# Moving three adaLN groups out of the expert routing in a four-layer diffusion step

## What is computed

```
mod = (silu(c) @ w_ada[i] + b_ada[i]).reshape(.., 6, D_MODEL)        # per layer i
h = rmsnorm(x, norm_mix[i]) * (1 + mod[1]) + mod[0];  x = x + mod[2] * mixer(h)
h = rmsnorm(x, norm_ffn[i]) * (1 + mod[4]) + mod[3];  x = x + mod[5] * moe(h)
moe: scores = sigmoid(h @ w_router); best group of four experts; two experts a token;
     y = sum_e combine[e] * (silu(h @ wg[e]) * (h @ wu[e])) @ wd[e]
```

## Time and profile before

| what | value |
|---|---|
| runs | 1558.07, 1559.05, 1563.91 us; median 1559.05 |
| the profiled execution | 1560.72 us, span 1558.6 us, 22820 instructions |
| TensorE (PE) busy | 1258.2 us, 81% of the span; granted clock 0.901 of full speed |
| VectorE, ScalarE, POOL busy | 362.8, 304.7, 165.8 us |
| DMA | 420.59 MB moved, mean 270 GB/s |
| queue q1 (SP's weights) | 331.37 MB, 54.3% of the 16 engines' span |
| queue q0 (POOL's) | 85.90 MB, 14.3% |
| chain that ended last | PE 60%, DMA 22%, VectorE 6%, issue 5%, POOL 3% |

### The profile page before, as it was taken

How to read it: one execution, slowest core, us unless ns; L and a number is a source line. 1 busy time by engine, 2 the same in 40 slices (tenths; PEclk the granted TensorE clock), 3 DMA queues, 4 the chain that set the end, 5 groups by cost and what they waited for, 6 DMA issues and landing times.

```text
span 1558.6 us, 22820 instructions
## 1 busy us (share of the span) xinstructions
PE 1258.2 (81%) x9738; PEld 729.6 (47%) x9738; DVE 362.8 (23%) x1127; ACT 304.7 (20%) x672; POOL 165.8 (11%) x231
## 2 busy tenths in 40 slices
PE   4889865799998999955798898889995567698756
PEld 2445432457865556522376433354652225464324
DVE  1442100230025234100121122223410004621003
ACT  1231100221136231100132112113110003311103
POOL 3001121200000000131200000000013120012210
PEclk8899987899999999987898999789998787899878
DMA  9999997933257758998741247605899875179952
GB/s 323 420 421 419 420 388 290 357 111 108 84 201 281 298 190 317 419 418 340 261 174 67 81 151 291 260 27 202 317 419 419 346 312 220 41 278 419 391 217 93
DMA packets 93266, 420.59 MB, mean 270 GB/s; under 512 B 12692, under 2 KB 38792, under 8 KB 52073
## 3 DMA queue, kind: packets, MB, share of 16 engines
q1 hardware_dynamic: 68048, 331.37, 54.3%
q0 software_dynamic: 24112, 85.90, 14.3%
q10 hardware_dynamic: 1000, 1.80, 0.3%
HBM read 418.93 MB, written 25.86 MB: 285 GB/s over the span
## 4 chain that ended last, share of the span: by engine, by line
PE 60%; DMA 22%; DVE 6%; issue 5%; POOL 3%; ACT 2%; SPq 1%; POOLq 0%; another core or an unknown queue 0%; ACTq 0%; DVEq 0%
PE bank L423 56%; DMA sb_ring<-in_w_exp_up,sb_spare 6%; DMA sb_ring<-in_w_exp_down,sb_spare 5%; DMA sb_ring<-in_w_exp_up 3%; POOL sb_ring L1963 2%; DMA sb_ring<-in_w_ada 2%; DMA sb_arena<-slot_out,sb_slots 2%; DMA slot_out<-sb_arena,sb_homes 1%; PE bank L868 1%; PE bank L800 1%; DMA sb_arena<-in_k_band 1%; POOL sb_arena L1984 1%; DMA sb_arena<-token_rows,sb_rows 1%; DVE sb_arena L1797 1%; SPq L410 1%
## 5 line engine op out<-in xcount | busy, mean ns | idle before, releaser
L423 PE MATMUL bank<-sb_ring,sb_arena 128*32 128x256 f32 (+1 forms) x5792 | 452.5, 447 | 152.8 <-DMA sb_ring<-in_w_exp_down,sb_spare 64.6
L423 PEld LDWEIGHTS bank<-sb_ring,sb_arena 128*32 128x32 f32 x5792 | 214.0, 115 | 360.7 <-issue 176.9
L423 PE MATMUL bank<-sb_arena 128*128 128x128 f32 (+8 forms) x600 | 110.6, 336 | 10.6 <-DVE sb_arena L1726 6.2
L423 PE MATMUL bank<-sb_ring,sb_hT 128*128 128x256 f32 x528 | 116.4, 383 | 2.6 <-ACT sb_hT L1087 2.6
L423 PE MATMUL bank<-sb_ring,sb_cond 128*2 128x512 f32 x768 | 102.0, 660 | 13.1 <-DMA sb_ring<-in_w_ada 12.3
L423 PEld LDWEIGHTS bank<-sb_ring,sb_hT 128*128 128x128 f32 x528 | 101.0, 192 | 17.9 <-issue 3.2
L423 PEld LDWEIGHTS bank<-sb_arena 128*128 128x128 f32 (+1 forms) x600 | 86.4, 203 | 37.7 <-issue 9.9
L1790 DVE TENSOR_TENSOR sb_arena<-sb_arena,bank 128x256 f32<-128x256 f32 x36 | 15.2, 421 | 345.2 <-PE bank L423 345.2
L423 PE MATMUL bank<-sb_arena,sb_ring 128*128 128x384 f32 (+2 forms) x288 | 94.3, 504 | 0.9 <-ACT sb_arena L1141 0.9
L423 PE MATMUL bank<-sb_hT,sb_ring 128*128 128x384 f32 x256 | 83.0, 486 | 0.7 <-DVE sb_hT L1608 0.7
L1797 DVE COPY sb_arena<-bank 128x512 f32<-128x512 f32 x36 | 24.9, 691 | 196.4 <-PE bank L423 196.4
...
## 6 DMA issues: line engine op xcount, KB each, us to landing
...
```

Source lines behind the costliest of these rows:

```text
L423: return pe.matmul(out, lhsT, rhs, start=first, stop=last)
```

## The change

The table `ADA_WINDOW` goes. Groups 3 and 7 (`ADA_TAIL`) are loaded behind the experts' units of layers 0 and 1 and multiplied in `combine`: four units between the products of the last round's outputs and the wait for the gathered rows, four behind the last of the 24 transposing products, in front of the next norm. Their transposes come behind that norm, the copy on ScalarE behind its squares, `mod_columns` ahead of VectorE's norm. Group 11 (`ADA_LATE`) is loaded behind layer 2's experts and multiplied in layer 3: four units at the start of the pooling mixer (behind the wait for `mix_in`), two behind the mixer, two and the transposes behind the second norm; group 2 of layer 0 keeps its place. Bank 7 stays with adaLN, so `combine` has seven banks: the eighth chunk shares bank 2 with the second, and its first product waits until VectorE has used that chunk (`x_ready`). `hold` moves on by eight units (`KC`) in all layers.

```diff
@@ -317,3 +317,4 @@
         ADA_MIXER = [(), (4, 5, 6), (8, 9, 10), ()]
-        ADA_WINDOW = [(3,), (7,), (11,), ()]
+        ADA_TAIL = [3, 7, None, None]
+        ADA_LATE = [2, None, None, 11]
         hold = {}
@@ -323,4 +324,3 @@
             if kind == 0:
-                if L == 0:
-                    ada_units(2)
+                ada_units(ADA_LATE[L])
             elif kind == 1:
@@ -348,6 +348,5 @@
             n_y += 8
-            ada_units(*ADA_WINDOW[L])
             moe_first.append(len(units))
 
-            hold[len(units) + 3 * (NE + SPARES) + 6] = (yg_in[NT - 1], 32 * (L + 1))
+            hold[len(units) + 3 * (NE + SPARES) + 6 + KC] = (yg_in[NT - 1], 32 * (L + 1))
 
@@ -371,2 +370,4 @@
             down_units(ROUNDS - 1)
+            if ADA_TAIL[L] is not None:
+                ada_units(ADA_TAIL[L])
 
@@ -380,3 +381,3 @@
 
-        COMBINE = [6, 2, 3, 1, 0, 7, 4, 5]
+        COMBINE = [6, 2, 3, 1, 0, 4, 5, 2]
 
@@ -536,2 +537,3 @@
                 else:
+                    ada(ADA_LATE[3], 0, 1, 2, 3)
                     project_group(r, 0)
@@ -832,5 +834,2 @@
                 ins.then_inc(pos_full, 1)
-                for g in ADA_WINDOW[L]:
-                    ada(g, 4, 5, 6, 7)
-
                 pe.wait_ge(slots_ready, 5 * L + 2)
@@ -848,5 +847,2 @@
                 ins.then_inc(pos_full, 1)
-                for g in ADA_WINDOW[L]:
-                    ada_columns(g)
-                    pe.wait_ge(mod_added, g + 1)
                 assert state["u"] == moe_first[L]
@@ -910,7 +906,16 @@
                     pe.wait_ge(ya_ready, R + ROUNDS)
-                    for c in (1, 2, 3, 0, 4, 5, 6, 7):
-                        if c == 0:
-                            pe.wait_ge(yb_ready, R + ROUNDS)
+                    def upper(c):
                         mm(bank[c][:, 0:TOK], ysb[:, 0, c * P:(c + 1) * P], last_a, True, False)
+
+                    for c in (1, 2, 3):
+                        upper(c)
+                    pe.wait_ge(yb_ready, R + ROUNDS)
+                    for c in (0, 4, 5, 6):
+                        upper(c)
+                    if ADA_TAIL[L] is not None:
+                        ada(ADA_TAIL[L], 0, 1, 2, 3)
                     for c in range(KC):
+                        if c == KC - 1:
+                            pe.wait_ge(x_ready, 8 * (n + 1) + 2)
+                            upper(c)
                         for t in range(NT):
@@ -920,2 +925,4 @@
                         ins.then_inc(yc_full, 1)
+                    if ADA_TAIL[L] is not None:
+                        ada(ADA_TAIL[L], 4, 5, 6, 7)
 
@@ -996,2 +1003,4 @@
                     norm(2 * L)
+                    if ADA_TAIL[L - 1] is not None:
+                        ada_columns(ADA_TAIL[L - 1])
                 (pool_mixer, mlstm, mla)[L % 3](2 * L)
@@ -1000,9 +1009,9 @@
                 if L == 0:
-                    ada(2, 0, 1, 2, 3, 4, 5)
+                    ada(2, 0, 1, 2, 3)
+                if ADA_LATE[L] is not None:
+                    ada(ADA_LATE[L], 4, 5)
                 norm(2 * L + 1)
-                if L == 0:
-                    ada(2, 6, 7)
-                    ada_columns(2)
-                for g in ADA_WINDOW[L]:
-                    ada(g, 0, 1, 2, 3)
+                if ADA_LATE[L] is not None:
+                    ada(ADA_LATE[L], 6, 7)
+                    ada_columns(ADA_LATE[L])
                 experts(L, 2 * L + 1)
@@ -1066,3 +1075,3 @@
 
-            def norm_scale(n):
+            def norm_scale(n, late=None):
                 if n and n % 2 == 0:
@@ -1074,2 +1083,4 @@
                     act.activation(sq[:, 2 * k:2 * k + 2, :], xT[:, 2 * k:2 * k + 2, :], ACT.Square).then_inc(sq_ready, 1)
+                if late is not None:
+                    mod_rows(late)
                 act.wait_ge(ms_full, n + 1)
@@ -1268,4 +1279,2 @@
                 tokens(0)
-                for g in ADA_WINDOW[L]:
-                    mod_rows(g)
                 silu(0)
@@ -1302,3 +1311,3 @@
                 if L:
-                    norm_scale(2 * L)
+                    norm_scale(2 * L, ADA_TAIL[L - 1])
                 act.wait_ge(mod_added, 3 * L + 1)
@@ -1312,4 +1321,4 @@
                 norm_scale(2 * L + 1)
-                if L == 0:
-                    mod_rows(2)
+                if ADA_LATE[L] is not None:
+                    mod_rows(ADA_LATE[L])
                 act.wait_ge(mod_added, 3 * L + 2)
@@ -1754,4 +1763,2 @@
                                        op0=ALU.add, op1=ALU.add).then_inc(slots_ready, 1)
-                for w in ADA_WINDOW[L]:
-                    mod_columns(w)
                 eq = rt[:, 20, :]
@@ -1871,2 +1878,4 @@
                 kind = L % 3
+                if L and ADA_TAIL[L - 1] is not None:
+                    mod_columns(ADA_TAIL[L - 1])
                 norm(2 * L, amp[:, L, 0, :, :])
@@ -1881,4 +1890,4 @@
                     mod_columns(ADA_MIXER[1][2])
-                if L == 0:
-                    mod_columns(2)
+                if ADA_LATE[L] is not None:
+                    mod_columns(ADA_LATE[L])
                 norm(2 * L + 1, amp[:, L, 1, :, :])
```

## The result

The changed kernel takes 1596.54 us (median of 4 runs, 1593.25 to 1598.91) where the kernel before, beside it on the same chip, takes 1558.56: a ratio of 1.0231, 95% interval 1.0196 to 1.0265, so 36 us slower. The profiled execution took 1596.69 us with a span of 1594.7, 36.1 more than before. The forecast was 1595. Its terms came out less exactly than their sum, and the rows show it. One execution of all that follow, of the version with the hold alone, took 2163.9 us at a mean granted clock of 0.549; the ratios leave it out, and why it was long stays open.

The account below looks back on a forecast made before the run. The prediction took DMA engines to bound expert stretches and TensorE with its helpers the mixers. Its terms summed to +35.6 us on the 1559.05 us median, 1594.7, rounded to 1595, with a range of 1570 to 1611.

Parts of the forecast that it names:

- What bounds the kernel: Whole kernel: DMA engines bound expert stretches, TensorE and its helpers bound mixers; the weight ring is full before the gate product.
- C: Behind layers 0 and 1: four adaLN units in front of the next norm add in full, twice, +7.6 us.
- D: Combine, all four layers: the eighth chunk's late product stands on the path, 0.67 us each, +2.7 us.
- A: Layer 0's experts: their stream starts with the ring full, as layer 3's does, -7.0 us; bounds -20 and 0.
- B: Last gathers of layers 0, 1, 2: more weight loads share the engines with them, +22.7 us (+4.3, +6.2, +12.2).
- E: Routing of layers 1 and 2: the 60 products run at the slow clock without adaLN work before them, +4.0 us.
- F: Layer 3's tables: loaded with the DMA engines to themselves, they arrive sooner, -2.6 us.
- G: Layer 3: group 11's units at the mixer's start and around the second norm are not hidden, +8.2 us.
- Gather last: Last gathers: they wait until all twelve weight units are through, +53 us in all, 1612 us; chance 0.12.
- hold harmless: Last gathers: the moved hold costs nothing, +13 us, 1572; chance 0.09, or 0.07 with layer 0's full gain, about 1559.
- weight queue decides: Everywhere: the weight queue sets the time and TensorE's work is hidden, -26.6 us, 1532 us; chance 0.06.
- rival 4: Combine: moved groups arrive late and TensorE waits for them, up to 10 us; given no chance of its own.

## Why the prediction was right

**What bounds the kernel** held: the ring was full before the first gate product in layers 0 and 1 (rows above), and adaLN products in front of a norm moved it by about their length (C and D).

**A** (layer 0's experts): forecast -7.0, measured +1.1 - 9.2 = -8.1. One profile flatters it, though. Over all profiles the stream takes 137.1 to 141.8 us with the group in front (mean 139.0 of six) and 127.6 to 137.1 without (mean 132.9 of seven), so the stream gains nearer 6 than 9 us, and A is nearer -5. The bound of -20 was far away. The spread among the seven has a place: the spare experts' up matrices, which POOL asks for 69.5 to 71.5 us into the stream, are used 92.1 to 96.3 us into it where it takes 127.6 to 132.4 us, and 100.0 to 101.4 us where it takes 135.3 to 137.1. Why they land later there stays open.

**B** (the last gather): forecast +22.7, measured +27.7 (6.1, 6.5, 15.2 against 4.3, 6.2, 12.2). The mechanism is shown three ways: the hold alone makes it, the hold put back removes it, the hold closed turns its sign. This is the term that was mis-sized. 3.4 of the 5.0 us are the stores ahead of the gather, which I left out: the gather's first instruction comes 22.1 us behind the down products in layer 0 instead of 19.1, half of that layer's loss, and 0.5 us later in layer 1. The gather itself (first instruction to last row) grew by 3.1, 6.0 and 15.2 us, so layer 2 is 3.0 over the forecast and layer 0 1.2 under. In layer 2, from 1297 to 1321 us, q1 sent 887 packets beside the gather's 861, where I had 818. That isn't more bytes (6.40 MB, and I had 6.7): I had counted 8.2 KB for each packet of a load, but 144 packets make a load of 1 MiB, 7.3 KB each. With that the same working would give layer 2 +11.1 and B about 21, further from what was measured. What the 22 us left out is an end below full rate: from 1315 to 1321 us 1.87 MB moved, 312 GB/s, where I had 420 GB/s to the last row.

**C and D**: forecast 7.6 + 2.7. Measured +4.5 in layer 0 and +4.2 in layer 1 (4.5 each forecast), +0.6 in layer 3; putting the units in the wait returned 3.7 and 3.5 of it, and the banks alone cost 0.6 to 0.8 a layer. In layer 2, where only D applies, last row to norm took 16.7 us against 16.8: its 0.7 us doesn't show in this profile.

**E** (routing clock): forecast 2.0 each in layers 1 and 2, measured 1.2 and 0.8. The start at clock 0.50 was right, and so was the cause, since products that keep the clock take it away. But I took layer 3's distance for both, 9.65 us from the start of the 60 products to the first expert product, where 9.37 and 8.41 were measured. In layer 2 that is the whole shortfall: the 60 products took 8.48 us, not 9.72. In layer 1 they took 9.44, with the clock back at 0.81 in their second half, and began 0.5 us sooner behind the norm (22.3 us instead of 22.9).

**F** (layer 3's tables): forecast -2.6, measured -2.8. From POOL's request to the products it takes 7.15 us, not 9.88. More weights beside the tables than before lengthen them by 6 us, which is the same mechanism from the other side.

**G** (group 11 in layer 3): forecast +8.2, measured +5.4. At the front the four units took 5.05 us, but the 24 products behind them 5.45 instead of 7.93: +2.6, where I had +3.8. I had charged 3.8 at full clock and credited nothing more, which was one row too coarse. Two units in front of the second norm cost their 1.9. For the two behind it I charged 2.5 us; VectorE's norm starts 7.0 us later, but the first expert product only 5.4: the 60 products begin 21.0 us behind the norm instead of 22.0 and take 9.12 us, not 9.72.

**Not forecast:** layer 2's mixer, +5.7 us. It needn't be the change's. The same stretch takes 287.9 us in the kernel before, 294.4 in the version that differs from it in layer 3 alone, and 285.6 to 293.6 in the others. Windows of 20 us, 230 us into that mixer, of the kernel before,

```profile
1020.34:1040.34 20.00, 15.32 (x47) 9.43 (x47) 4.71 (x14) 2.32 (x6) 0.00 (x0) 0.83 0.00 1
```

of the changed kernel,

```profile
1033.93:1053.93 20.00, 15.46 (x38) 9.52 (x38) 3.97 (x12) 2.32 (x6) 0.00 (x0) 0.55 0.00 1
```

and of the version with 12 products in layer 3,

```profile
1019.96:1039.96 20.00, 15.47 (x36) 9.15 (x35) 3.96 (x12) 2.32 (x6) 0.00 (x0) 0.52 0.00 1
```

show the granted clock at 0.83, 0.55 and 0.52 with the same idle share. Which level a profile meets there changes from one execution to the next, and what decides it stays open.

**The sum.** A to G measured come to 33.6 us, against 35.6 forecast: B 5.0 over, and A, C and D, E, F and G together 7.0 under. The other 2.5 of the 36.1 us are stretches that I had put at nothing: layer 2's mixer +5.7, layer 1's mixer -1.6, the rest -1.6. So the mechanisms were right and so was the size of most terms, but that the total came within 2 us is luck: errors of 5 and 7 us went opposite ways.

**The rivals.** Gather last falls with the hold alone in layer 0, hold harmless with layers 1 and 2 of the same run, and weight queue decides with the empty window from 117 to 121 us. The late units (rival 4) didn't appear in the changed kernel; they do where all eight stand ahead of the wait.
